# Rotary embedding by column order: q and k columns split into halves, scores on 32 rows, heads in pairs

## The reference

```python
def apply_rope(t, cos, sin):
    t1, t2 = jnp.split(t, 2, axis=-1)
    return jnp.concatenate([t1 * cos - t2 * sin, t2 * cos + t1 * sin], axis=-1)
...
    qkv = (x @ w_qkv).reshape(B, T, 3, H, Dh)
    q, k, v = [jnp.transpose(qkv[:, :, n], (0, 2, 1, 3)).astype(f32) for n in range(3)]
    cos, sin = rope_tables(T)
    q = apply_rope(q, cos, sin) * (Dh ** -0.5)
    k = apply_rope(k, cos, sin)
...
    s_own = jnp.einsum('bhqd,bhsd->bhqs', q_c, k_own)
    s_own = jnp.where(causal, s_own, -jnp.inf)
    p = jax.nn.softmax(jnp.concatenate([s_sel, s_own], axis=-1), axis=-1)
```

## Time and profile before

| | us |
|---|---|
| median of 3 runs | 1218.9 (1217.95 to 1219.27) |
| the profiled execution | 1219.48 |
| its span | 1217.7 |
| TensorE busy | 1180.7 (97%) |
| VectorE busy | 752.7 (62%) |
| ScalarE busy | 617.7 (51%) |
| GpSimd busy | 109.5 (9%) |

### The profile page before, as it was taken

How to read it: one execution, slowest core, us unless ns; L and a number is a source line. 1 busy time by engine, 2 the same in 40 slices (tenths; PEclk the granted TensorE clock), 3 DMA queues, 4 the chain that set the end, 5 groups by cost and what they waited for, 6 DMA issues and landing times.

```text
span 1217.7 us, 24847 instructions
## 1 busy us (share of the span) xinstructions
PE 1180.7 (97%) x10598; PEld 1064.5 (87%) x10598; DVE 752.7 (62%) x1084; ACT 617.7 (51%) x892; POOL 109.5 (9%) x87
## 2 busy tenths in 40 slices
PE   6999999999999999999999999999999999999997
PEld 6797777789999989997999999799988898999996
DVE  7788775374554467785555444758478564655554
ACT  8974543363434355554643434565545474644443
POOL 0032253601100000220010000000000000000000
PEclk9999989999999999999999999999999999999999
DMA  8522111055544545333455446354432352545551
GB/s 297 209 104 72 27 53 52 20 196 217 193 186 180 206 168 183 129 119 124 173 197 186 178 169 255 109 186 173 152 126 105 138 191 104 206 177 206 188 185 42
DMA packets 29950, 188.17 MB, mean 155 GB/s; under 512 B 3489, under 2 KB 5665, under 8 KB 8737
## 3 DMA queue, kind: packets, MB, share of 16 engines
q1 hardware_dynamic: 27072, 177.21, 39.9%
q10 hardware_dynamic: 2784, 9.60, 2.4%
HBM read 185.75 MB, written 1.05 MB: 153 GB/s over the span
## 4 chain that ended last, share of the span: by engine, by line
PE 86%; DVE 8%; ACT 4%; issue 2%; DMA 0%; ACTq 0%; DVEq 0%; SPq 0%
PE ps L2046 24%; PE ps L2048 24%; PE ps L2047 23%; DVE w_lo L1333 1%; PE ps L2364 1%; PE ps L2179 1%; PE ps L2509 1%; PE ps L2369 1%; PE ps L2542 1%; PE ps L2366 1%; ACT mixed L618 1%; ACT w_hi L720 1%; PE ps L2312 1%; PE ps L2263 1%; PE ps L2762 1%
## 5 line engine op out<-in xcount | busy, mean ns | idle before, releaser
L1333 DVE TENSOR_TENSOR w_lo<-w_raw,w_hi 128x2048 fp32r<-128x2048 f32 x157 | 365.7, 2345 | 147.4 <-ACT w_hi L589 146.8
L2046 PE MATMUL ps<-x_hi,w_hi 128*128 128x256 f32 x1344 | 380.3, 283 | 4.1 <-DVE x_lo L1620 2.4
L2047 PE MATMUL ps<-x_lo,w_hi 128*128 128x256 f32 x1344 | 375.3, 279 | 0.0
L2048 PE MATMUL ps<-x_hi,w_lo 128*128 128x256 f32 x1344 | 375.1, 279 | 0.0
L589 ACT CAST w_hi<-w_raw 128x2048 fp32r<-128x2048 f32 x155 | 295.1, 1906 | 155.0 <-PE ps L2048 154.0
L2046 PEld LDWEIGHTS ps<-x_hi,w_hi 128*128 128x128 f32 x1344 | 252.6, 188 | 13.3 <-issue 8.3
L2047 PEld LDWEIGHTS ps<-x_lo,w_hi 128*128 128x128 f32 x1344 | 252.6, 188 | 2.2 <-issue 0.7
L2048 PEld LDWEIGHTS ps<-x_hi,w_lo 128*128 128x128 f32 x1344 | 252.6, 188 | 0.0
L2046 PE MATMUL ps<-w_hi,hid_hi 128*128 128x512 f32 x304 | 119.7, 394 | 0.1
L2048 PE MATMUL ps<-w_hi,hid_lo 128*128 128x512 f32 x304 | 119.4, 393 | 0.0
L2047 PE MATMUL ps<-w_lo,hid_hi 128*128 128x512 f32 x304 | 118.5, 390 | 0.0
(11 more groups left out here) (394 smaller groups left out, 1797.5 us busy)
## 6 DMA issues: line engine op xcount, KB each, us to landing
w_raw<-in_weights SPq DMA_DIRECT2D x163, 1024.0 KB, 4.9
xt<-in_xT SPq DMA_DIRECT2D x2, 512.0 KB, 5.4
w_raw<-in_weights SPq DMA_DIRECT2D x2, 512.0 KB, 6.2
x_tm<-in_x SPq DMA_DIRECT2D x1, 1024.0 KB, 5.2
gain<-in_mix_g ACTq DMA_DIRECT2D x2, 512.0 KB, 4.0
gain<-in_mix_b ACTq DMA_DIRECT2D x2, 512.0 KB, 6.0
gain<-in_ffn_g ACTq DMA_DIRECT2D x2, 512.0 KB, 7.7
gain<-in_ffn_b ACTq DMA_DIRECT2D x2, 512.0 KB, 10.8
```

Of the source, the lines that this page charges most:

```text
L1333: V.tensor_tensor(w_lo[:, i % WS, :], w_raw[:, i % RAW, :], w_hi[:, i % WS, :].bitcast(F32), ALU.subtract).then_inc(lo_done, 1)
L2046: nc.tensor.matmul(out, hi_l, hi_r, start=start, stop=False)
L2047: nc.tensor.matmul(out, hi_l, lo_r, start=False, stop=False)
L2048: return nc.tensor.matmul(out, lo_l, hi_r, start=False, stop=stop)
```

## The change

The columns of each q and k slab of MoBA are put in another order when the slab is rounded: of the four heads' 4 x 64 columns the first halves of all heads (4 x 32) come first, then the second halves. `HALVES` names these eight slabs; for them `hi`, `hi_half` and `lo` work in two pieces, which read runs of 32 numbers and write runs of 128. Feature tile m of q and k is then half m of all four heads, head h on partitions 32h to 32h + 31. `rope` finds the partner half in the other tile, so that `rotate`, its matrix and its semaphore go; it has a buffer `rt` each for q and k, waits for ScalarE's copy (`p_taken`) and reads SBUF alone. `moba_scores` adds up two products on 32 rows for each head and token half, the four heads next to each other in the order. `moba_outputs`, `fx_scores` and `fx_outputs` take heads 0 and 1, then 2 and 3, in turns; `moba_outputs` waits for its bank to be taken (`o_taken`) and no longer for `rope_done`.

```diff
@@ -288,13 +281,13 @@
-            ma_q, ma_k, ma_q2, ma_k2, rt = (sb(n, [P, 2, T], where=a) for n in
-                                                  ("ma_q", "ma_k", "ma_q2", "ma_k2", "rt"))
+            ma_q, ma_k, ma_q2, ma_k2, rt_q, rt_k = (sb(n, [P, 2, T], where=a) for n in
+                                                  ("ma_q", "ma_k", "ma_q2", "ma_k2", "rt_q", "rt_k"))
-            rope_c = sb("rope_c", [P, 2 * T + P], where=a)
+            rope_c = sb("rope_c", [P, 2 * T], where=a)
...
@@ -334,6 +327,16 @@
             eng.wait_ge(lo_done, i + 1 + r * per)
+        HALVES = [first["qkv"] + 3 * g + n for g in range(4) for n in range(2)]
+        def halves_first(w, m):
+            return w.rearrange("p (k h m f) -> p k h m f", h=4, m=2, f=HD // 2)[:, :, :, m]
+        def halves_placed(w, m):
+            return w.rearrange("p (k m h f) -> p k m h f", m=2, h=4, f=HD // 2)[:, :, m]
         def wview(w, i, kind):
...
@@ -586,6 +589,11 @@
                     act.wait_ge(slab_done, i - WS + 1 + r * per)
+                if i in HALVES:
+                    for m in range(2):
+                        ins = nc.scalar.copy(halves_placed(w_hi[:, i % WS, :], m), halves_first(w_raw[:, i % RAW, :], m))
+                    ins.then_inc(hi_done, 1)
+                    return
                 nc.scalar.copy(w_hi[:, i % WS, :], w_raw[:, i % RAW, :]).then_inc(hi_done, 1)
...
@@ -717,7 +725,11 @@
                 at = slice(1024 * q, 1024 * q + 1024)
-                ins = nc.scalar.copy(w_hi[:, i % WS, at], w_raw[:, i % RAW, at])
+                if i in HALVES:
+                    for m in range(2):
+                        ins = nc.scalar.copy(halves_placed(w_hi[:, i % WS, at], m), halves_first(w_raw[:, i % RAW, at], m))
+                else:
+                    ins = nc.scalar.copy(w_hi[:, i % WS, at], w_raw[:, i % RAW, at])
                 if q:
...
@@ -1330,6 +1342,12 @@
                 dve.wait_ge(hi_done, i + 1 + r * per)
+                if i in HALVES:
+                    for m in range(2):
+                        ins = V.tensor_tensor(halves_placed(w_lo[:, i % WS, :], m), halves_first(w_raw[:, i % RAW, :], m),
+                                              halves_placed(w_hi[:, i % WS, :], m).bitcast(F32), ALU.subtract)
+                    ins.then_inc(lo_done, 1)
+                    return
                 V.tensor_tensor(w_lo[:, i % WS, :], w_raw[:, i % RAW, :], w_hi[:, i % WS, :].bitcast(F32),
...
@@ -1816,10 +1834,12 @@
             def rope(g, n):
-                src, dst, c = ((ma_q, ma_q2, HD ** -0.5), (ma_k, ma_k2, 1.0))[n]
-                dve.wait_ge(rot_ready, 2 * g + n + 1)
+                src, dst, rt, c = ((ma_q, ma_q2, rt_q, HD ** -0.5), (ma_k, ma_k2, rt_k, 1.0))[n]
+                if g:
+                    dve.wait_ge(rope_done, 2 * g + n - 1)
+                dve.wait_ge(p_taken, 3 * g + n + 1)
                 for m in range(2):
-                    V.scalar_tensor_tensor(rt[:, m, :], ps[:, 3, T * m:T * m + T], c, sin, ALU.mult, ALU.mult)
+                    V.scalar_tensor_tensor(rt[:, m, :], src[:, 1 - m, :], c if m else -c, sin, ALU.mult, ALU.mult)
                     ins = V.scalar_tensor_tensor(dst[:, m, :], src[:, m, :], c, cos, ALU.mult, ALU.mult)
...
@@ -2515,19 +2535,6 @@
             transposes(1, ((0, 0), (1, 7), (1, 4)))
-            def rotate(g, n):
-                if g == 0 and n == 0:
-                    pe.wait_ge(late_loaded, 80)
-                if g > 1 and n == 0:
-                    pe.wait_ge(o_taken, g - 1)
-                if n or g:
-                    pe.wait_ge(rope_done, 2 * g + n)
-                pe.wait_ge(p_taken, 3 * g + n + 1)
-                mm(ps[:, 3, :], rope_c[:, 2 * T:2 * T + P], (ma_q, ma_k)[n][:, :, :].rearrange("p a b -> p (a b)"),
-                   start=True, stop=True).then_inc(rot_ready, 1)
             def moba_project(g, n):
...
@@ -2536,11 +2543,13 @@
                     pe.wait_ge(pt_taken, 4 * g)
-                for s, h in enumerate(HEADS):
-                    q, m = head(h)
-                    for t, c0, c1 in CAUSAL:
-                        last = mm(ps[:, 4 + s, c0:c1], ma_q2[q, m, tok(t)], ma_k2[q, m, 0:c1 - c0], start=True, stop=True)
-                    last.then_inc(scores_ready, 1)
+                for t, c0, c1 in CAUSAL:
+                    for m in range(2):
+                        for h in range(4):
+                            f = slice(HD // 2 * h, HD // 2 * h + HD // 2)
+                            last = mm(ps[:, 4 + h, c0:c1], ma_q2[f, m, tok(t)], ma_k2[f, m, 0:c1 - c0], start=m == 0, stop=m == 1)
+                            if t and m:
+                                last.then_inc(scores_ready, 1)
             def moba_transposes(g):
...
@@ -2548,14 +2557,14 @@
                 bank = 3 if g < 3 else 4
-                if g < 3:
-                    pe.wait_ge(rope_done, 2 * g + 4)
-                for s, h in enumerate(HEADS):
-                    q, m = head(h)
-                    pe.wait_ge(pt_taken, 4 * g + s + 1)
-                    v = lambda t: ma_vv[:, g % 2, t, HD * h:HD * h + HD]
-                    mm(ps[q, bank, T * m:T * m + T], v(0), ma_p[:, s, 0:T], start=True, stop=False)
-                    last = mm(ps[q, bank, T * m + P:T * m + T], v(1), ma_p[:, s, T:T + P], start=False, stop=True)
+                if 0 < g < 3:
+                    pe.wait_ge(o_taken, g)
+                for m in range(2):
+                    pe.wait_ge(pt_taken, 4 * g + 2 * m + 2)
+                    for t in range(TT):
+                        for h in (2 * m, 2 * m + 1):
+                            last = mm(ps[head(h)[0], bank, T * m + P * t:T * m + T], ma_vv[:, g % 2, t, HD * h:HD * h + HD],
+                                      ma_p[:, h, T * t:T + P * t], start=t == 0, stop=t == 1)
                 last.then_inc(o_ready, 1)
...
@@ -2563,16 +2572,12 @@
                 moba_project(0, n)
-                if n:
-                    rotate(0, n - 1)
             moba_project(1, 0)
             for g in range(3):
                 moba_scores(g)
                 moba_project(g + 1, 1)
-                rotate(g + 1, 0)
                 moba_project(g + 1, 2)
                 moba_transposes(g)
-                rotate(g + 1, 1)
                 if g < 2:
...
@@ -2659,24 +2664,27 @@
                     pe.wait_ge(o_taken, O_FX + 1)
-                for s, h in enumerate(HEADS):
-                    q, m = head(h)
+                for m in range(2):
                     for t, c0, c1 in CAUSAL:
-                        last = mm(ps[:, 4 + s, c0:c1], fx_q[q, 2 * g + m, tok(t)], fx_k[q, 2 * g + m, 0:c1 - c0],
-                                  start=True, stop=True)
-                    last.then_inc(scores_ready, 1)
+                        for h in (2 * m, 2 * m + 1):
+                            q = head(h)[0]
+                            last = mm(ps[:, 4 + h, c0:c1], fx_q[q, 2 * g + m, tok(t)], fx_k[q, 2 * g + m, 0:c1 - c0],
+                                      start=True, stop=True)
+                            if t:
+                                last.then_inc(scores_ready, 1)
...
```

26 lines of the change are left out of this document (10 added, 16 removed).

## The result

The kernel after takes 1203.3 us (median of five executions, 1201.6 to 1208.6), the one before 1217.95 (five, 1215.6 to 1219.3): a ratio of 0.989, 95% interval 0.987 to 0.992, so by the ratio 13.1 us less, 10 to 16 (the two medians lie 14.6 apart).

A forecast was written before the change was run, and what follows sets the result against it. TensorE was taken to bound the MoBA stage, VectorE close behind. Gains less stalls, group by group, plus 0.7 in forgetting attention, made 12.0 us off the median 1218.9: forecast 1207.0, own range 1204.8 to 1209.2, to 1211.9 with rivals 1 to 3.

The forecast's parts named there:

- Scores: MoBA scores on 32-row quarters, four at a time: 1.49 us a group instead of 2.27, gain 3.1 us for four groups.
- Rival 3: MoBA scores: quarters overlap by half only, each head's second pass holding the next back; 2.8 us a group, 1211.7; chance 0.09.
- rival 4: MoBA scores: products on 32 rows run one at a time, 5.4 us a group, 1222.6, slower than before; chance 0.04.
- Outputs: MoBA outputs issued in pairs of heads: 1.45 us a group instead of 2.15, gain 2.8 us for four groups.
- Rotating products: MoBA, TensorE: the products that rotated q and k go, 0.86 us each, two a group, 6.9 us in all.
- Splits: MoBA q and k slabs split in two pieces on ScalarE and VectorE: hidden mostly, 0.3 us added at slab qkv+1.
- rival 2: MoBA slab splitting: strided halves cost half as much again for each element, +1 us on both engines, 1211.8; chance 0.10.
- Group 1's factors: VectorE's softmax factors in MoBA's group 1 end 14.7 us after the scores began, stalling TensorE's transposes by 0.8 us.
- Distances: Times between the starts of successive MoBA groups' scores: 21.3, 22.1 and 20.9 us.
- Rival 1: MoBA: no stalls, VectorE and ScalarE catch up; 12.8 us less 0.3 come through, 1 us more later, 1205.2; chance 0.14.
- Forgetting attention: Stage after MoBA: only the second outputs count, 0.70 us gained, bounds 0.5 and 3; the rest lost waiting for VectorE.
- Rival 5: The change doesn't do what it says: pairs don't overlap, only the rotating products pay, about 1213; chance 0.04.

The follow-up runs named there:

- rot_back: Changed kernel with eight products of the rotating product's size put back, results unused and waited for by nobody: the MoBA stage loses 4.4 to 4.55 us.
- pool_late: Changed kernel with GpSimd's MoBA products begun only after VectorE has split the slab they met: stage gain 12.4 us, 0.75 more than with GpSimd at its old place.
- fx_old: Changed kernel with the forgetting attention's scores and outputs as before, head by head: 0.88 us more from the norm behind the MoBA stage to the end.

## Why the prediction was wrong in its time and right in its mechanism

**The step that failed** is the one from the sum to the range: "The profiled execution took 1219.5 us (span 1217.7), so 1207.5 (span 1205.7); it lies 0.6 above the median 1218.9, whence 1206.9", and "Its own range: 1204.8 to 1209.2", with terms for stalls, scores and the forgetting attention and none for the executions themselves: how much they differ was put at nothing, and "A measurement of this kernel tells 0.2%, 2.4 us, from no change" says the same. Three runs that agreed within 1.3 us stood for a kernel whose executions spread over 11.6. The half-rate stretches were in the trace of before, and I read the clock only in the MoBA stage, where it was 1.00. A change of 12.0 from 1218.9 gives 1206.9; the 11 executions of the kernel after have their median at 1205.7, and the five that were compared at 1203.3, three of these five with a clock of 0.997 or 0.998, where four of eleven have that. So of the 3.7 us between forecast and result 2.4 are which executions were drawn. The other 1.3 lie between the forecast and the median of the 11; the aligned starts put 0.6 of them down to the sum, which was too small (12.0 for 12.6), and for the rest no run shows a cause. The range was also narrower than its own terms: stalls gone (0.8 and 0.4) and 2 us more in the forgetting attention make 3.2 us below 1206.9, so 1203.7 and not 1204.8. That would still not have reached 1203.3.

**Point by point.**
- Scores: taken at 1.49 (bounds 1.49 and 5.4), measured 1.52, which is 3.4 times less than the 5.17 estimated for one after the other. The 3.07x of the Trainium skill (TensorE: Matmul & The Clock Gate, Part 3, measured speedup), given there for 512 columns, would have made it 1.9; these products of 128 and 256 columns did better. That the products alternate between the quarters was what mattered (3.17 us head by head); the prediction didn't price it.
- Rival 3 (each head's second pass holding back the next) and rival 4 (one at a time) fell: the four heads start within 0.02 us (473.000, 473.007, 473.013, 473.020).
- Outputs: 1.45 against 1.45.
- Rotating products: 6.9 us of TensorE's time. `rot_back` loses 4.4 to 4.55 of them: 1.7 before the first scores, 1.67, 0.92 and 0.24 in the three distances. The rest disappears in the stalls of groups 1 and 2 and in the last wait, which the prediction's sum also took off, group by group.
- Splits: 0.19 at slab qkv+1 instead of 0.3; rival 2 fell.
- Group 1's factors, 14.7 us after the scores and measured 14.6: right in part by luck. The sum has "the split adds 0.34; about 0.3 comes back", so a slab of some 3.27 us. It took 3.61, because its second piece waits about 1 us for GpSimd, which `pool_late` shows. What came back was 0.6 us, in the four maxima and not in the slab: GpSimd was through earlier, and from the first of them to the q rotation it is 3.42 us (500.88 to 504.30) where it was 4.03 (509.62 to 513.65 in the earlier trace rows).
- Distances: predicted 21.3, 22.1 and 20.9; measured 21.42, 22.26 and 20.56. Stall at group 1's transposes 0.8, measured 0.88; wait before the last scores "about 2", measured 1.72. Rival 1 (no stalls) fell, though its time is the nearest to the result: it names 1205.2, and its terms (12.5 us in MoBA, 0.7 and 1 more later) make 1204.7. That it lies near is luck, for the stalls are there.
- Forgetting attention: 0.7, measured 0.88 by `fx_old` and 0.97 by the first pair of traces.
- Sum 12.0, measured 12.6 by the traces. The stage has 11.65 where I had 11.3, 0.2 better ahead of the first scores and 0.3 at group 2, 0.1 worse at each of groups 0 and 1; the forgetting attention has 0.2 to 0.3 more.
- Rival 5 ("only the rotating products pay") fell. Taken singly, putting back the rotating products costs 4.5 us, the old outputs 2.05, the old wait 1.9; with four times 0.75 for the scores (2.27 less 1.52) that makes 11.4 of the stage's 11.65. Each of the three was measured with the others in place, and the scores' share is a difference of lengths: no run puts the old scores back.

## What to carry to other kernels

Before a forecast of under 1%, look at the granted clock over the whole span and not in the changed stage only, and give the range a term for it; three runs that agree say little. Compare two versions by the starts of instructions that are the same in both, ahead of the changed stage and behind it: this gave the change within some tenths of a us from single executions of a kernel whose whole times spread over 7, as long as no half-rate stretch fell into the stage (one moved it by 1.5).

Products on quarters of the rows paid here only where the quarter changed after one or two products: that took 1.52 and 1.64 us, three and four in a row 2.50 and 3.17, against 2.27 on the halves before.

When TensorE gets faster in a stage, put what it waits for next first in VectorE's order; two moved calls were worth another 2.9 us here.
